# Cached keys turned by VectorE from a block layout that the page gather writes, with each sequence's values moved behind the next sequence's logits

## The chip, the cores and the metric

One core of a Trainium2 chip runs the whole program. The metric is device time in microseconds, of which less is better, as the median of the runs shown.

## What is computed

A two-layer decoder trunk is applied to 512 prompt tokens and to a sample group of 8 sequences with 4 new tokens each, with shared weights. Each layer has one wide input projection, sparse attention, a causal depthwise convolution branch, gates, and an output projection. The change touches only the attention of the sample group. Its cached keys and values lie in pages of 128 tokens; a page table gives 16 pages to each sequence. Cut to that part, for sequence by sequence:

```
k_past = cache_k[l][page_table].reshape(8, 2048, 2, 128)      # 16 pages of 128 tokens, 2 key heads of 128
v_past = cache_v[l][page_table].reshape(8, 2048, 2, 128)
ki_past = cache_kidx[l][page_table].reshape(8, 2048, 64)      # indexer keys, for the top-k choice
s = einsum('btkgd,btnkd->btkgn', q, k_all[idx]) * 128 ** -0.5 # idx: the top 256 keys of each query
o = einsum('btkgn,btnkd->btkgd', softmax(s), v_all[idx])
```

The kernel computes logits against all 2052 keys and adds a bias of -1e30 where a key is not among the top 256, which gives the same result. All data are float32.

## The kernel before

**The frame.** `half_chunk` (L1180) is the frame of everything: per layer 59 column tiles `n` of 256 columns, each in 4 chunks `i` of 512 rows, each chunk in two halves `m`. SP loads a chunk of weights (512 KB) into `raw`, ScalarE makes its high part `w_hi_t` (L882), GpSimd its low part `w_lo_t` (L869), and TensorE (PE) runs 24 float32r products of 272 columns per half. `raw` holds four chunks; SP loads chunk m when GpSimd has finished chunk m - 4.

**The asides.** Everything else is hung behind these halves by tables of step numbers. From tile 11 (`N_GLU`) to tile 42 the steps are numbered h = 0 to 255, one per half, and each engine's `window(l, h)` holds what it does behind that half, in its own program order. The engines meet by semaphores only. The queue of SP is also one program order: `load_weights(m)`, then the `aside` of chunk m - 4, which issues all other transfers.

**The sample attention** starts at h = 200 (`H_AS`) and takes 6 steps (`A_STEP`) per sequence b. With s = 200 + 6b:

- s+0, s+1, s+3, s+4 (`turn_at`): `turn_k` on PE turns a quarter of the keys (4 pages, 512 tokens, 2 heads) by 8 transposes of 128x128 into PSUM (L1377). ScalarE (L1055) and VectorE (`keep_k`, L1848) each copy one head from PSUM into `k_t`. The quarter comes from `k_ring`, a ring of three loads of 512 KB (L633); quarter q may be loaded once quarter q - 3 has been turned.
- s+5 (`logits_at`): `logits_s` multiplies the blocked queries with `k_t` (L1392) and with the new keys (L1395); VectorE (L1854) and ScalarE (L1058) make the softmax.
- s+7 (`pturn_at`): `turn_s` transposes the probabilities (L1402), behind the same half as `turn_k` of the next sequence's second quarter.
- s+8 (`values_at`): `values_s` multiplies them with the values (L1412, L1414) into bank 3 of `aux`; VectorE copies the result out (`keep_o`, L1867). Then SP may load the next sequence's four `v_page` tiles (L638), for which it waits in its queue.

**The gather.** `gather` (L640 to L645) runs in the asides of SP in earlier tiles: it reads a page number into a register and copies that page from the cache to a near DRAM tensor, as it lies, in 16 runs of 8 KB for a page of keys or values. In layer 0, tiles 1 to 16 gather the indexer keys of both layers (two pages per chunk), tiles 17 to 32 the keys and values of layer 0; in layer 1, tiles 1 to 16 gather the keys and values of layer 1. Each k or v page is 128 KB.

Of the kernel before, what the change touches and what calls it, by code (L numbers as in the profile page):

```python
# [5 lines left out]
F32 = mybir.dt.float32  # L6
# [300 lines left out]
def values_at(b):  # L307
    return logits_at(b) + 3
# [28 lines left out]
def trunk_kernel(nc, x_prompt, x_sample, c_prompt, c_sample, cache_k, cache_v, cache_kidx, state_conv, page_table,  # L337
# [4 lines left out]
    with ExitStack() as ctx:  # L342
# [4 lines left out]
        k_near = nc.dram_tensor("k_near", [DEPTH, SEQS, PAGES, PAGE, KVW], F32).ap()  # L347
# [77 lines left out]
        k_ring = at(C + 16512, "k_ring", [P, 3, 4, KVW])  # L425
# [10 lines left out]
        k_t = at(C + 11072, "k_t", [P, 4, KVH, 512])  # L436
# [53 lines left out]
        def ada_place(d):  # L490
# [14 lines left out]
            k_landed0 k_landed1 k_landed2 k_turned k_cp_a k_cp_b logits_s brep_in0 brep_in1 sraw_done exp_s ps_ready pts_ps pts_done  # L505
# [42 lines left out]
        def _(sp):  # L548
# [64 lines left out]
            def load_kx(l, b):  # L613
                if b < 2:
                    sp.wait_ge(S.q_blocked, 2 * l + 1)
                    sp.wait_ge(S.dots_ready, len(PACKS) * (l + 1))
                    sp.wait_ge(S.kx_staged, 16 * DEPTH * SEQS * PAGES)
# [7 lines left out]
            def load_k(l, q):  # L625
# [7 lines left out]
                sp.dma_start(k_ring[:, q % 3], k_near[l, b, 4 * j:4 * j + 4].rearrange("g p c -> p g c")).then_inc(k_landed[q % 3], 16)  # L633
# [6 lines left out]
            def gather(places, staged):  # L640
# [107 lines left out]
            def aside(l, n, i):  # L748
# [7 lines left out]
                kv = [(near[l], cache[l].rearrange("g p h d -> g p (h d)")) for near, cache in ((k_near, cache_k), (v_near, cache_v))]  # L756
# [119 lines left out]
        def _(act):  # L876
# [101 lines left out]
            def window(l, h):  # L978
# [67 lines left out]
                for b in range(SEQS):  # L1046
                    for j in range(4):
                        if h == turn_at(b, j):
                            q = 32 * l + 4 * b + j
                            act.wait_ge(S.k_turned, q + 1)  # L1050
                            if b >= 1:
                                act.wait_ge(S.logits_s, 8 * l + b)
# [1123 lines left out]
```

## Time and profile before

| | |
|---|---|
| median of 3 runs | 3469.86 us (3469.58 to 3471.81) |
| profiled execution | 3463.73 us, span 3461.9 us |
| PE busy | 3381.8 us, 98% of the span |
| VectorE, GpSimd, ScalarE busy | 1828.8, 1238.4, 1047.1 us |
| granted TensorE clock, mean | 0.987 |
| DMA | 593.09 MB, 171 GB/s in the mean |

Busy time of an engine is the time in which the hardware profiler saw it work on an instruction. Matmuls are pipelined: one that starts every 0.25 us is shown with a duration of 0.41 us. The cost of a group of matmuls is therefore read from the starts of its neighbours, not from its own duration. A DMA share is the part of the time in which the core's 16 DMA engines worked on packets.

### The profile page before, as it was taken

The page shows a single profiled execution, that of the slowest core. Times are in us where ns is not written, and L with a number is a line of the kernel's source. Part 1 is how long each engine was busy: PE and PEld are TensorE (multiplying, and loading weights), DVE is VectorE, ACT ScalarE, POOL GpSimd, SP SyncE. Part 2 cuts the span into 40 slices and gives each one's busy share as a digit, 9 for nine tenths or more (in the row PEclk, how much of TensorE's full clock was granted, in tenths as well). Part 3 has the DMA queues.
Part 4 walks back from the last instruction along what each step waited for, and adds up shares of the span by engine and source line. Part 5 has one row for each costly group of instructions (what it writes and reads, how often), then busy time and mean ns, then how long its engine had stood idle before and what let it go on. Part 6 is the DMA issues. An engine that isn't in the chain of part 4 may idle for free. (4 is left out here: it accounts for less than half of the span.)

```text
span 3461.9 us, 66254 instructions
## 1 busy us (share of the span) xinstructions
PE 3381.8 (98%) x27454; PEld 3161.4 (91%) x27454; DVE 1828.8 (53%) x2535; ACT 1047.1 (30%) x1444; POOL 1238.4 (36%) x508
## 2 busy tenths in 40 slices
PE   5899999999999999999999999999999999999999
PEld 2699989989999989998888999898999998899998
DVE  1524468999986123342226244789989841233211
ACT  2322322223542333222223222322235423332211
POOL 0243333446324223333333333334462332234433
PEclk8899999999999999999999999999999999999999
DMA  9844444666545774658895666544332257644444
GB/s 325 283 108 117 109 112 121 188 180 200 155 133 163 232 240 157 210 194 288 289 296 177 182 174 181 141 129 114 102 112 77 84 186 237 219 149 135 131 130 95
DMA packets 591304, 593.09 MB, mean 171 GB/s; under 512 B 110876, under 2 KB 556337, under 8 KB 580923
## 3 DMA queue, kind: packets, MB, share of 16 engines
q1 hardware_dynamic: 588732, 588.59, 56.7%
q8 instruction: 216, 3.54, 0.4%
q14 instruction: 84, 0.69, 0.1%
q10 hardware_dynamic: 2272, 0.28, 0.1%
HBM read 546.37 MB, written 116.39 MB: 191 GB/s over the span
## 5 line engine op out<-in xcount | busy, mean ns | idle before, releaser
L869 POOL TENSOR_TENSOR w_lo_t<-raw,w_hi_t 128x1024 fp32r<-128x1024 f32 x472 | 1193.3, 2529 | 2199.4 <-ACT w_hi_t L882 2199.4
L1180 PE MATMUL acc<-act_hi,w_hi_t 128*128 128x272 f32 x6528 | 1390.0, 294 | 18.2 <-POOL w_lo_t L869 9.7
L1180 PE MATMUL acc<-act_hi,w_lo_t 128*128 128x272 f32 x6528 | 1353.0, 289 | 0.0
L1180 PE MATMUL acc<-act_lo,w_hi_t 128*128 128x272 f32 x6528 | 1349.5, 288 | 0.0
L1180 PEld LDWEIGHTS acc<-act_hi,w_hi_t 128*128 128x128 f32 x6528 | 1028.2, 189 | 77.4 <-issue 55.7
L1180 PEld LDWEIGHTS acc<-act_lo,w_hi_t 128*128 128x128 f32 x6528 | 1028.5, 189 | 0.0
L1180 PEld LDWEIGHTS acc<-act_hi,w_lo_t 128*128 128x128 f32 x6528 | 1022.6, 189 | 0.0
L882 ACT ACTIVATE w_hi_t<-raw 128x1024 fp32r<-128x1024 f32 x472 | 499.9, 1059 | 1645.1 <-PE acc L1180 1631.5
L1757 DVE SCALAR_TENSOR_TENSOR conv<-conv,cw 128x512 f32<-128x512 f32 x240 | 236.1, 984 | 13.6 <-POOL w_lo_t L869 13.6
L1180 PE MATMUL acc<-m_hi,w_hi_t 128*128 128x272 f32 x1024 | 215.2, 292 | 0.0
L1180 PE MATMUL acc<-m_lo,w_hi_t 128*128 128x272 f32 x1024 | 211.5, 287 | 0.0
L1180 PE MATMUL acc<-m_hi,w_lo_t 128*128 128x272 f32 x1024 | 211.4, 287 | 0.0
L1757 DVE SCALAR_TENSOR_TENSOR d_odd<-conv,cw,d_odd 128x512 f32<-128x512 f32 x224 | 196.9, 879 | 12.7 <-POOL w_lo_t L869 12.6
L1658 DVE TENSOR_TENSOR stage<-stage,cs 128x544 f32<-128x544 f32 x38 | 39.5, 1041 | 310.2 <-DMA stage<-stage 310.2
L1848 DVE COPY k_t<-aux 128x512 f32<-128x512 f32 x64 | 44.3, 692 | 242.9 <-PE aux L1377 242.9
L1180 PEld LDWEIGHTS acc<-m_hi,w_hi_t 128*128 128x128 f32 x1024 | 159.6, 188 | 4.1 <-issue 4.1
L1180 PEld LDWEIGHTS acc<-m_lo,w_hi_t 128*128 128x128 f32 x1024 | 161.3, 188 | 0.0
L1180 PEld LDWEIGHTS acc<-m_hi,w_lo_t 128*128 128x128 f32 x1024 | 160.1, 188 | 0.0
L1799 DVE MAX8 top<-work_s 32x8 f32<-32x2052 f32 x62 | 141.5, 2282 | 0.9
L1801 DVE MATCH_REPLACE8 work_s<-top,work_s 32x2052 f32<-32x2052 f32 x62 | 140.6, 2268 | 0.0
L2052 DVE SCALAR_TENSOR_TENSOR x_v<-acc,mod,x_old 128x544 f32<-128x544 f32 x32 | 25.1, 783 | 197.2 <-PE acc L1180 181.0
L2033 DVE TENSOR_TENSOR gates<-acc,gates 128x544 f32<-128x544 f32 x32 | 23.2, 725 | 166.8 <-PE acc L1180 166.8
(244 smaller groups left out, 2599.2 us busy)
## 6 DMA issues: line engine op xcount, KB each, us to landing
raw<-in_w_in_dram SPq DMA_DIRECT2D x272, 512.0 KB, 3.8
ada_ring<-in_w_ada_dram SPq DMA_DIRECT2D x95, 512.0 KB, 7.0
raw<-in_w_in_dram SPq DMA_DIRECT2D x136, 256.0 KB, 3.3
k_near<-in_cache_k_dram SPq DMA_DIRECT2D x256, 128.0 KB, 2.7
v_near<-in_cache_v_dram SPq DMA_DIRECT2D x256, 128.0 KB, 2.7
k_ring<-k_near SPq DMA_DIRECT2D x64, 512.0 KB, 5.2
v_page<-v_near SPq DMA_DIRECT2D x64, 512.0 KB, 6.4
raw<-in_w_out_dram SPq DMA_DIRECT2D x64, 512.0 KB, 4.3
```

The source lines that it names most:

```text
L869: pool.tensor_tensor(w_lo_t[:, m % 2], raw[:, m % 4], w_hi_t[:, m % 2].bitcast(F32), ALU.subtract).then_inc(S.w_lo, 1)
L882: act.activation(w_hi_t[:, m % 2], raw[:, m % 4], ACT.Copy).then_inc(S.w_hi, 1)
L1180: last = pe.matmul(acc[:, 2 * m + h, 0:HALF], w[:, c % 2, k, P * m:P * m + P], r[:, kt, h * HALF:(h + 1) * HALF], start=first and k == 0 a ...
L1658: st.then(dve.tensor_tensor(x, x, cs[:, cos, :], ALU.mult))
L1757: st.then(dve.scalar_tensor_tensor(out=out, in0=src, scalar=w, in1=out, op0=ALU.mult, op1=ALU.add))
L1799: st.then(dve.max(top8[0:NS, :], src))
L1801: st.then(dve.match_replace(work_s[:, :], top8[0:NS, :], src, NEG))
L1848: dve.tensor_copy(k_t[:, j, 1, :], aux[:, 1, :]).then_inc(S.k_cp_b, 1)
L2033: dve.tensor_tensor(pair(gates[:, 2 + m, :]), accv(m), pair(gates[:, 2 + m, :]), ALU.mult).then_inc(acc_free[m], 1)
L2052: st.then(dve.scalar_tensor_tensor(out=pair(x_v[:, k, :]), in0=accv(m), scalar=g[:, 0:1], in1=pair(old), op0=ALU.mult, op1=ALU.add))
```

## The change

- The near key tensor of a page is laid out as (head, block a of 32 dimensions, token, 32 dimensions). The gather writes a key page so, with 1024 pieces of 32 floats (128 bytes), where it copied 16 runs of 8 KB.
- The key pages of each layer are gathered one per chunk in tiles 1 to 32 (`page_at`). Tiles 1 to 16 also gather that layer's own indexer keys, tiles 17 to 32 its values, two pages per chunk. So both layers gather in the same way.
- A load into `k_ring` puts token group k and block a on partition 32a + k, in 1024 pieces of 512 bytes, where it had 512 pieces of 1 KB. One VectorE instruction (`dve.transpose`, 32x32 blocks, 128 partitions by 1024 elements) turns a quarter straight from `k_ring` into `k_t`. The transposes of PE, the two copies out of PSUM and their semaphores go.
- `values_at(b)` becomes `logits_at(b + 1)`, three steps later, behind the same half as the next sequence's logits (for the last one, two steps later). The values are made in bank 0 of `aux`, which the key turns have left; `logits_s` waits no more for `o_done`.

Its core (lines of the changed kernel's neighbours are cut):

```diff
 def values_at(b):
-    return logits_at(b) + 3
+    return logits_at(b + 1) if b < SEQS - 1 else logits_at(b) + 5
...
+def page_at(n, i):
+    return divmod(4 * (n - 1) + i, PAGES)
...
-        k_near = nc.dram_tensor("k_near", [DEPTH, SEQS, PAGES, PAGE, KVW], F32).ap()
+        k_near = nc.dram_tensor("k_near", [DEPTH, SEQS, PAGES, KVH, HD // BLK, PAGE, BLK], F32).ap()
...
-                sp.dma_start(k_ring[:, q % 3], k_near[l, b, 4 * j:4 * j + 4].rearrange("g p c -> p g c")).then_inc(k_landed[q % 3], 16)
+                src = k_near[l, b, 4 * j:4 * j + 4].rearrange("y g a (k m) i -> (a k) (y g) (m i)", m=PAGE // BLK)
+                sp.dma_start(k_ring[:, q % 3], src).then_inc(k_landed[q % 3], 16)
...
+                    if keys is not None:
+                        near, cache = keys
+                        sp.dma_start(near[b, g].rearrange("h a k i -> (h a) k i"),
+                                     cache[ds(page, 1)].rearrange("y k (c i) -> (y c) k i", i=BLK)).then_inc(S.kv_staged, 16)
...
-                if l == 0 and 1 <= n < 17:
-                    gather([(x, [(kx_near[a], cache_kidx[a]) for a in range(DEPTH)]) for x in staged_at(n, i)], S.kx_staged)
-                if l == 0 and 17 <= n < 33:
-                    gather([(x, kv) for x in staged_at(n - 16, i)], S.kv_staged)
-                if l > 0 and 1 <= n < 17:
-                    gather([(x, kv) for x in staged_at(n, i)], S.kv_staged)
+                if 1 <= n < 33:
+                    gather([(page_at(n, i), [])], S.kv_staged, keys)
+                if 1 <= n < 17:
+                    gather([(x, [(kx_near[l], cache_kidx[l])]) for x in staged_at(n, i)], S.kx_staged)
+                if 17 <= n < 33:
+                    gather([(x, [values]) for x in staged_at(n - 16, i)], S.kv_staged)
...
-                            act.activation(k_t[:, j, 0, :], aux[:, 0, :], ACT.Copy).then_inc(S.k_cp_a, 1)
...
-                for g in range(KVH):
-                    for kk in range(4):
-                        last = pe.transpose(aux[:, g, P * kk:P * kk + P], k_ring[:, q % 3, kk, g * HD:(g + 1) * HD], ident)
-                last.then_inc(S.k_turned, 1)
...
-                dve.tensor_copy(k_t[:, j, 1, :], aux[:, 1, :]).then_inc(S.k_cp_b, 1)
+                dve.transpose(k_t[:, j].rearrange("p x (k m) -> p x m k", m=PAGE // BLK),
+                              k_ring[:, q % 3].rearrange("p x (m i) -> p x m i", i=BLK)).then_inc(S.k_turned, 1)
```

**How it moves instructions.** PE, in the sample attention of layer 0, from the second sequence's first key turn to its logits; the rows of the projection (L1180, in the changed kernel L1181) are left out. Before:

```order
L1377 MATMUL aux<-con,k_ring 128x128 [waits k_cp_b,k_cp_a,k_landed1]
...
L1402 MATMUL aux<-con,probs_s 128x128 [waits ps_ready]
...
L1377 MATMUL aux<-con,k_ring 128x128 [waits k_cp_b,k_cp_a,k_landed2]
...
L1412 MATMUL aux<-v_page0,pt_s 32x256 [waits v_landed2,v_landed1,v_landed3,v_landed0,pts_done]
...
L1377 MATMUL aux<-con,k_ring 128x128 [waits k_cp_b,k_cp_a,k_landed0]
...
L1392 MATMUL aux<-k_t,q_blk 32x512 [waits pts_done,q_blocked,o_done,k_cp_b,k_cp_a]
```

The same stretch in the changed kernel:

```order
L1389 MATMUL aux<-con,probs_s 128x128 [waits ps_ready]
L1389 MATMUL aux<-con,probs_s 128x128 x3
L1390 MATMUL aux<-con,p_tail 32x128
...
L1379 MATMUL aux<-k_t,q_blk 32x512 [waits pts_done,q_blocked,k_turned]
L1379 MATMUL aux<-k_t,q_blk 32x512 x7
L1382 MATMUL aux<-k_new,q_blk 32x4 x8
L1401 MATMUL aux<-v_page0,pt_s 32x256 [waits v_landed1,v_landed2,v_landed0,v_landed3,praw_done,pts_done]
```

The four key turns are gone, and the values of the first sequence stand directly behind the logits of the second, with no projection between them.

SP, in the same part of the program, over one sequence. Before:

```order
L633 DMA k_ring<-k_near 128x4x256 [waits k_turned] x2
L638 DMA v_page<-v_near 128x4x256 [waits pv_s,ao_p] x2
L660 DMA gate_spill<-gate 128x544 [waits acc0_free]
L573 DMA raw<-in_w_in_dram 128x4x256 [waits w_lo]
L633 DMA k_ring<-k_near 128x4x256 [waits k_turned]
L638 DMA v_page<-v_near 128x4x256 [waits pv_s,ao_p] x2
```

In the changed kernel:

```order
L639 DMA k_ring<-k_near 128x8x128 [waits k_turned]
L644 DMA v_page<-v_near 128x4x256 [waits pv_s,ao_p] x4
L578 DMA raw<-in_w_in_dram 128x4x256 [waits w_lo]
L665 DMA bias_s<-bias_spill 32x1x512 [waits sraw_done]
L665 DMA bias_s<-bias_spill 32x1x512 x2
L665 DMA bias_s<-bias_spill 32x1x516
L639 DMA k_ring<-k_near 128x8x128 [waits k_turned] x2
```

The four loads of values now go out together, 2 MB ahead of the next weights and of the next two loads of keys.

## Rows read from the trace of the kernel before

**Rows 1.** The page, part 1, and the weight split's row of part 5.

```profile
PE 3381.8 (98%) x27454; PEld 3161.4 (91%) x27454; DVE 1828.8 (53%) x2535; ACT 1047.1 (30%) x1444; POOL 1238.4 (36%) x508
...
L869 POOL TENSOR_TENSOR w_lo_t<-raw,w_hi_t 128x1024 fp32r<-128x1024 f32 x472 | 1193.3, 2529 | 2199.4 <-ACT w_hi_t L882 2199.4
```

**Rows 2.** Groups by line: engine, op, tiles, shapes, count; busy us, mean ns; idle before.

```profile
L1377 PE MATMUL aux<-con,k_ring 128*128 128x128 f32 x512 | 66.3, 273 | 0.0
...
L1848 DVE COPY k_t<-aux 128x512 f32<-128x512 f32 x64 | 44.3, 692 | 242.9 <-PE aux L1377 242.9
...
L2063 DVE STREAM_TRANSPOSE y_t<-x_v 128x512 f32<-128x512 f32 x16 | 11.4, 711 | 0.5
```

**Rows 3.** Timeline of PE around one key turn: start us, duration us, line.

```profile
1154.43 0.41 PE L1180 MATMUL acc<-act_lo,w_hi_t 128*128 128x272 f32 x2
1154.68 0.42 PE L1180 MATMUL acc<-act_hi,w_lo_t 128*128 128x272 f32 x2
1154.93 1.04 PE L1377 MATMUL aux<-con,k_ring 128*128 128x128 f32 x8
1155.72 0.49 PE L1180 MATMUL acc<-act_hi,w_hi_t 128*128 128x272 f32 x2
1156.06 0.42 PE L1180 MATMUL acc<-act_lo,w_hi_t 128*128 128x272 f32 x2
```

**Rows 4.** Timeline of PE around the values of one sequence.

```profile
1175.90 0.41 PE L1180 MATMUL acc<-act_hi,w_lo_t 128*128 128x272 f32 x2
1176.24 1.93 PE L1412 MATMUL aux<-v_page,pt_s 128*32 128x256 f32 x32
...
1178.65 0.52 PE L1180 MATMUL acc<-act_hi,w_hi_t 128*128 128x272 f32 x2
1179.00 0.41 PE L1180 MATMUL acc<-act_lo,w_hi_t 128*128 128x272 f32 x2
```

**Rows 5.** Stretches: length, busy of PE, PEld, DVE, ACT, POOL, granted clock, DMA share, GB/s.

```profile
2821.00:3044.00 223.00, 223.00 (x2032) 201.60 (x2032) 41.80 (x91) 80.45 (x116) 61.72 (x26) 1.00 0.74 236
1169.00:1196.00 27.00, 27.00 (x251) 24.14 (x250) 4.44 (x11) 10.67 (x16) 7.16 (x3) 1.00 0.77 246
1570.00:1770.00 200.00, 198.62 (x1849) 175.49 (x1848) 62.28 (x90) 42.38 (x58) 62.42 (x26) 1.00 0.95 312
```

**Rows 6.** DMA queue in 2685 to 2745 us: packets, MB, share of 16 engines.

```profile
q1 hardware_dynamic: 3600, 4.26, 24.1%
```

**Rows 7.** DMA in 1858 to 1955 us; issues: count, KB each, median us to landing.

```profile
q1 hardware_dynamic: 10620, 17.38, 61.0%
...
k_near<-in_cache_k_dram SPq DMA_DIRECT2D x30, 128.0 KB, 2.8
```

**Rows 8.** DMA in 400 to 573 us.

```profile
q1 hardware_dynamic: 31754, 17.78, 39.0%
...
raw<-in_w_in_dram SPq DMA_DIRECT2D x48, 256.0 KB, 3.3
```

**Rows 9.** DMA in 3256 to 3440 us.

```profile
q1 hardware_dynamic: 47600, 22.49, 45.9%
...
out_dram<-y_t SPq DMA_DIRECT2D x56, 64.0 KB, 2.0
```

**Rows 10.** DMA in 1115 to 1333 us.

```profile
k_ring<-k_near SPq DMA_DIRECT2D x29, 512.0 KB, 4.8
...
raw<-in_w_in_dram SPq DMA_DIRECT2D x25, 512.0 KB, 6.9
```

**Rows 11.** SP's waits in 1115 to 1335 us: us in total, times, longest.

```profile
SPq L573 <- POOL w_lo_t L869: 56.6, 16, 7.4
```

**Rows 12.** Timeline of SP over one weight chunk in layer 1.

```profile
2007.75 0.38 SPq L573 DMA_DIRECT2D raw<-in_w_in_dram  x1
2008.90 0.51 SPq L645 DMA_DIRECT2D k_near<-in_cache_k_dram  x1
...
2013.77 0.38 SPq L573 DMA_DIRECT2D raw<-in_w_in_dram  x1
```

More of the change, by code:

```diff
@@ L435, in trunk_kernel @@
         z_t = at(C + 21176, "z_t", [SEQS, NS])
-        k_t = at(C + 11072, "k_t", [P, 4, KVH, 512])
+        k_t = at(C + 11072, "k_t", [P, 4, 4 * KVH, PAGE])
         bias_s = [at(C + 23456, "bias_s0", [P, 516]), at(C + 15176, "bias_s1", [P, 516])]
@@ L638, in load_v, with gather @@
                 sp.dma_start(v_page[j][:, :, :], v_near[l, b, 4 * j:4 * j + 4].rearrange("g p c -> p g c")).then_inc(v_landed[j], 16)
-            def gather(places, staged):
+            def gather(places, staged, keys=None):
                 for (b, g), targets in places:
@@ L755, in aside @@
                     sp.dma_start(mask_t[:, :, :, :], table[:, T_MASK:N_TAB].rearrange("p (a b n) -> p a b n", a=2, b=SEQS)).then_inc(S.cs_in, 16)
[L756 to L762 removed]
+                keys, values = ((near[l], cache[l].rearrange("g p h d -> g p (h d)")) for near, cache in ((k_near, cache_k), (v_near, cache_v)))
+                if 1 <= n < 33:
[4 more added lines that the diff above has]
+                    gather([(x, [values]) for x in staged_at(n - 16, i)], S.kv_staged)
                 if 1 <= n <= N_GLU and i < 2:
@@ L1046, in window @@
                 for b in range(SEQS):
[L1047 to L1052, printed above, removed]
-                            else:
-                                act.wait_ge(S.bias_stored, 16 * l + 16)
-                            act.activation(k_t[:, j, 0, :], aux[:, 0, :], ACT.Copy).then_inc(S.k_cp_a, 1)
                     if h == logits_at(b):
@@ L1388, in logits_s @@
                     pe.wait_ge(S.pts_done, 8 * l + b)
-                    pe.wait_ge(S.o_done, 8 * l + b)
                 for g in range(KVH):
                     for j in range(4):
-                        pe.matmul(aux[32 * j:32 * j + 32, 2, :], q_blk[:, b, g, :], k_t[:, j, g, :], start=g == 0, stop=g == 1)
+                        pe.matmul(aux[32 * j:32 * j + 32, 2, :].rearrange("p (y n) -> p y n", n=PAGE), q_blk[:, b, g, :], k_t[:, j, g:4 * KVH:KVH, :], start=g == 0, stop=g == 1)
                 for g in range(KVH):
@@ L1457, in window @@
                 for b in range(SEQS):
+                    if h == pturn_at(b):
+                        turn_s(l, b)
+                    if h == logits_at(b):
+                        logits_s(l, b)
+                for b in range(SEQS):
                     if h == values_at(b):
                         values_s(l, b)
-                    if h == pturn_at(b):
-                        turn_s(l, b)
-                    for j in range(4):
-                        if h == turn_at(b, j):
-                            turn_k(l, b, j)
-                    if h == logits_at(b):
-                        logits_s(l, b)
                 if h == H_COMB:
@@ L1840, in turn_q, with turn_k @@
                 last.then_inc(S.q_blocked, 1)
-            def keep_k(l, b, j):
-                dve.wait_ge(S.k_turned, 32 * l + 4 * b + j + 1)
+            def turn_k(l, b, j):
+                q = 32 * l + 4 * b + j
+                dve.wait_ge(k_landed[q % 3], 16 * (q // 3 + 1))
                 if b >= 1:
@@ L1866, in keep_o @@
                 dve.wait_ge(S.pv_s, 8 * l + b + 1)
-                dve.tensor_copy(o_part[b][:, :], aux[:, 3, 136:136 + KVW]).then_inc(S.o_done, 1)
+                dve.tensor_copy(o_part[b][:, :], aux[:, 0, 0:KVW]).then_inc(S.o_done, 1)
             def peaks(l):
@@ L1968, in window @@
                         if h == turn_at(b, j):
-                            keep_k(l, b, j)
+                            turn_k(l, b, j)
+                for b in range(SEQS):
                     if h == values_at(b):
```

22 lines of the change are left out of this document (8 added, 14 removed).

## The prediction

> **What bounds the kernel now.** I read the page first. PE is busy 98% of the span; VectorE, GpSimd and ScalarE have 36 to 53% [rows 1]. Then the stretch of the sample attention in layer 1: PE is busy for all 223 of 223 us, at a granted clock of 1.00, with VectorE at 41.8 us and a DMA share of 0.74 [rows 5]. So what leaves PE's queue there leaves the time, as long as nothing else is late; and the nearest thing to a second bound is DMA, not an engine. The timeline then prices a group of matmuls by its neighbours' starts, and the DMA views price packets by their length.
>
> **What leaves PE.** The projection starts a pair of products every 0.25 us (1154.43 to 1154.68). Around a key turn the last pair before starts at 1154.68, the first two after at 1155.72 and 1156.06 [rows 3]: 1.38 us where two steps of 0.25 would be, so the turn costs 0.88 us, and 0.09 of that is the slow first step when the projection comes back (0.34 for 0.25). There are 4 x 8 x 2 = 64 turns. Fourteen of them (the second quarter of sequences 1 to 7, twice) share their half with the transposes of the probabilities, which stay and keep that 0.09; they give 0.79. The sum is 50 x 0.88 + 14 x 0.79 = **55.1 us**. It can't be more than the 66.3 us that the group shows as busy, since that counts the overlap [rows 2], and hardly less than 64 x 0.70 = 45, if every turn kept an entry and an exit of 0.09.
>
> **The values behind the logits.** The values pay 0.34 for 0.25 before their first matmul and 0.35 for 0.25 behind their last [rows 4]: 0.19 us of switching. Behind the next logits they share that group's entry and exit; the last sequence's share those of the peak transposes. 16 x 0.19 = **3.0 us**; at worst nothing. Their own matmuls stay. `logits_s` loses its wait for `o_done` and the values keep it; PE had no wait here to lose, so this is worth nothing by itself.
>
> **What VectorE takes over.** The nearest row is a block transpose of 128 x 512 at 711 ns [rows 2]; twice that, 1.42 us, is my value for 128 x 1024. The new one writes with a stride, which no row shows; 2.8 us is my upper end, 0.7 the lower. A sequence has 4 of them in place of 4 copies of 0.69: 4 x (1.42 - 0.69) = +2.9 us on 4.44 busy in 27 [rows 5], +8.4 at the upper end. Both are hidden: four turns must fit between two logits, some 23 us apart. VectorE now waits for `k_landed` itself; behind such a wait stand the softmax and the copy of the values, which PE needs one or two halves later. ScalarE loses its copies; nobody waited for them. Nothing of this counts.
>
> **What DMA takes over.** First the price of a byte. With mostly weights in flight, 60 us x 0.241 x 16 engines = 231 engine-us moved 4.26 MB: 54.3 ns per 1000 bytes [rows 6]. With pages going from DRAM to DRAM in 8 KB runs it is 97 x 0.61 x 16 / 17.38 = 54.5, the same [rows 7]. Then the price of a cut. Where the weights come in 24576 pieces of 512 bytes (48 x 256 KB), 173 x 0.39 x 16 = 1080 engine-us stand against 17.78 x 54.3 = 965: 4.6 ns more per piece [rows 8]. Where the outputs go in 28672 pieces of 128 bytes (56 x 64 KB), it is 1351 against 1221: 4.5 ns [rows 9].
>
> - A load of keys: 28.5 engine-us for its bytes, plus 1024 x 4.6 = 4.7: 2.07 us of the 16 engines where it had 1.78. A sequence needs 0.77 x 27.0 = 20.8 us of DMA now [rows 5], then 20.8 + 4 x 0.29 = 22.0. Its PE time falls to 27.0 - 3.5 - 0.2 = 23.3. The share rises to 94%. That is much, but a stretch with a share of 0.95 has PE at 198.6 of 200 us [rows 5]. Cost: nothing.
> - A gathered key page: 7.1 + 4.7 = 11.8 engine-us, 0.74 us in place of 0.45. No row shows 128-byte pieces from DRAM to DRAM; I take rows 9 and use as upper end a 1 KB packet's price, 55.6 ns per piece, so 3.6 us per page. A chunk lasts 6.02 us [rows 12] and needs 1.78 for weights, 0.74 for the page and 0.2 for two indexer pages, or 0.9 for two value pages: under 3.5 us, and 5.6 to 6.2 at the upper end, where the chunks of tiles 17 to 32 also hold asides of PE. Cost: nothing, with room up to (6.0 - 2.0) x 16 / 1024 = 62 ns per piece.
> - SP's queue: a gathered copy takes 0.51 us and the reading of a page number about 0.77 (2008.13 to 2008.90); a chunk of 6.02 us held two readings and four copies [rows 12], 3.6 us. Now it is three and three, 3.8 us. In the sample attention SP still stood 56.6 us waiting for weights to be split [rows 11], so it is not late.
> - The burst: four value loads (7.1 us), a chunk of weights (1.8), bias rows (under 1) and then the fourth quarter of the keys (2.1), which would land some 13 to 14 us after the preceding values; its turn is needed after six halves, 6 x 3.0 + 0.7 = 18.8 us. It fits by about 4 us. The weights have four chunks of ring, some 20 us, against landings of 6.9 us [rows 10].
>
> **Sum.** -55.1 - 3.0 = -58.1 us. The profiled execution has 3463.73 us and becomes 3405.6; it is 6.1 below the median of the runs shown, so the median becomes 3469.9 - 58.1 = **3411.8 us**, 1.7% less. The likeliest case's own ends are 3408 (a little more of the switching goes) and 3422 (the low end of the turns).
>
> **Rival 1: DMA becomes the bound of the sample attention.** It decides once a sequence needs more than 23.3 us, so once a 512-byte piece costs over (28.5 + 0.62 x 16) / 1024 = 37.5 ns, against 32.4 by rows 8. For it: only 14% of margin, weight landings of 6.9 us there [rows 10] where the halves of a chunk took 3.3 earlier [rows 8], and the burst. Against it: the 0.95 stretch. Halfway, at 24.8 us per sequence, 16 x 1.5 = 24 us are lost: 3436. At the full price of a 1 KB packet a load takes 3.56 us and a sequence 27.9: slower than now by 16 x 0.9 = 14 us, 3484.
>
> **Rival 2: the gather in 128-byte pieces is too dear.** This is the slower side. It decides from 62 ns per piece. At twice a 1 KB packet's price, 111 ns, a page takes 7.1 us and a chunk 9.1, where the chunks last 3462 / 472 = 7.3 us in the mean [rows 1]; over 256 chunks that is +460 us, about 3870. Against it: stores of 128-byte pieces cost 11.5 ns each [rows 9]. For it: those go from SBUF, while here both ends are DRAM and the reads jump by 1 KB. The Trainium skill (DMA: Bandwidth & Descriptors, Specifications) says that below 512 bytes a transfer is done as read-modify-write; that would be such a mechanism, though on the stores of rows 9 no such price is seen.
>
> **Rival 3: the copy falls apart into single floats.** If a rearranged copy were moved element by element, 32 packets of 4.6 ns and the bytes make 154 ns per piece, 9.9 us per page, 11.9 per chunk, +1180 us: 4590. Against it: both sides have runs of 32 floats, and the weights' cut to 512 bytes cost a piece's price, not an element's. The Trainium skill (VectorE: DVE Perf Modes, The three transpose paths) warns that a plain copy whose access pattern makes the transpose is 19 times slower when the innermost destination stride is large. Here the innermost stride is one element, so I read the rule as not meeting this case; 19 times 0.45 us would be 8.5 us per page.
>
> **Chances.** Forecast 0.78, rival 1 0.14 (mostly between 3420 and 3450), rival 2 0.06, rival 3 0.01, anything else 0.01. A measurement of this kernel tells about 0.2% (7 us) from no change. Faster by more than that: the forecast and most of rival 1, 0.90. Within it: a part of rival 1, 0.03. Slower: rivals 2 and 3 and the far end of 1, 0.07. The range 3407 to 3440 holds the forecast with its ends and the nearer half of rival 1.
>
> **What would show it.** In the changed profile the group of key transposes is absent, PE is still busy for all of the sample attention, a sequence takes 23.3 us (that stretch 26 to 28 us shorter per layer), the other stretches last as long as before, and the DMA share there is about 0.9. The block transposes show 1.3 to 1.5 us; over 3 the estimate is wrong, over 4 PE waits for them. Rival 1 would show waits of PE for `k_t`, `v_page` or `w_lo_t` there and a share near 1. Rivals 2 and 3 would show the chunks of tiles 1 to 32 longer than before, with PE waiting for weights. A gain under 45 us with no new wait would mean that I misprice a turn.

## The result and the profile after

The changed kernel takes 3446.57 us (median of 4 runs, 3442.52 to 3450.13) against 3470.84 us for the kernel before on the same chip. The ratio is 0.9927, 95% interval [0.9912, 0.9943]: 24 us faster, where 58 were forecast, and outside the range given. The profiled execution has 3449.85 us, span 3448.0. That is 3.3 us above its median, and the profiled execution before was 7.1 below its own (3463.73, span 3461.9), so the two traces differ by 13.9 us where the medians differ by 24.3. What follows on single stretches is from the traces.

First the page of the changed kernel (parts 1 and 5), beside [rows 1] and [rows 2].

```profile
PE 3342.3 (97%) x26942; PEld 3116.9 (90%) x26942; DVE 1919.6 (56%) x2535; ACT 1012.8 (29%) x1380; POOL 1241.7 (36%) x508
...
L1181 PE MATMUL acc<-act_hi,w_hi_t 128*128 128x272 f32 x6528 | 1388.2, 294 | 37.8 <-POOL w_lo_t L879 14.1
...
L1645 DVE TENSOR_TENSOR stage<-stage,cs 128x544 f32<-128x544 f32 x38 | 41.1, 1082 | 336.2 <-DMA stage<-stage 336.2
...
L1837 DVE STREAM_TRANSPOSE k_t<-k_ring 128x1024 f32<-128x1024 f32 x64 | 124.6, 2021 | 135.3 <-DMA k_ring<-k_near 135.0
```

The 512 transposes are gone from PE. But PE's idle time ahead of the projection is 37.8 us; here is the same row of the kernel before:

```profile
L1180 PE MATMUL acc<-act_hi,w_hi_t 128*128 128x272 f32 x6528 | 1390.0, 294 | 18.2 <-POOL w_lo_t L869 9.7
```

**Where the gain is.** Windows of the changed kernel, with the columns of [rows 5]; the last two lie in the sample attention of layer 0 and of layer 1, the first in tile 5 and the second in tile 12 of layer 0.

```profile
246.00:260.00 14.00, 10.84 (x74) 10.43 (x73) 6.00 (x6) 2.19 (x3) 4.91 (x2) 0.90 0.47 114
...
437.00:468.00 31.00, 28.55 (x200) 27.79 (x201) 14.91 (x28) 5.47 (x6) 9.25 (x4) 0.83 0.51 132
1162.00:1260.00 98.00, 98.00 (x910) 87.20 (x909) 41.23 (x45) 32.04 (x45) 30.86 (x13) 1.00 0.91 269
2866.00:2960.00 94.00, 94.00 (x878) 83.20 (x878) 37.91 (x43) 30.42 (x41) 28.73 (x12) 1.00 0.92 267
```

In the sample attention PE is busy for all of the time at a granted clock of 1.00, and DMA has a share of 0.91 to 0.92: as forecast. The first two windows are of another kind. Before, they read as follows; the second lies there in tiles 12 and 13, since the kernel before reaches tile 12 at 424.5 us already and has PE busy for all of its 26.8 us.

```profile
246.00:260.00 14.00, 14.00 (x114) 14.00 (x113) 0.83 (x1) 3.26 (x4) 6.77 (x3) 1.00 0.45 114
...
437.00:468.00 31.00, 31.00 (x246) 29.92 (x245) 17.19 (x29) 7.61 (x9) 13.13 (x5) 1.00 0.45 116
```

**The map of the time.** GpSimd's 472 splits of weights (`w_lo_t`) are a clock of the program: the time from the first split of one tile to the first of a later tile is the length of the tiles between. In us, from the profiled executions (layer 0 / layer 1):

| tiles | before | after | e1 | e3 | e2 |
|---|---|---|---|---|---|
| 5 | 24.1 / 24.1 | 29.2 / 29.2 | 24.1 / 24.1 | 24.1 / 24.1 | 24.1 / 24.1 |
| 6 | 25.9 / 25.9 | 30.7 / 28.1 | 25.9 / 25.9 | 25.9 / 25.9 | 25.9 / 25.9 |
| 7 to 10 | 102.8 / 102.8 | 104.8 / 104.8 | 102.8 / 102.8 | 102.8 / 102.8 | 102.8 / 102.8 |
| 11 to 16 | 174.8 / 174.8 | 183.4 / 183.1 | 174.8 / 174.8 | 174.8 / 174.8 | 174.8 / 174.8 |
| 19 to 26 | 222.6 / 224.1 | 226.3 / 225.1 | 222.6 / 224.1 | 223.6 / 225.3 | 226.4 / 229.9 |
| 27 to 30 | 122.2 / 122.2 | 122.2 / 122.2 | 122.2 / 122.2 | 122.2 / 122.2 | 127.8 / 129.4 |
| 33 to 42 | 311.7 / 311.5 | 283.1 / 282.7 | 283.0 / 283.0 | 282.9 / 283.7 | 283.2 / 283.5 |

Tiles 33 to 42 hold the sample attention: 28.6 and 28.8 us shorter, 57.4 together. Tiles 5 to 26 are 24.2 and 18.6 us longer, 42.8 together. So the gain is there in full, and in these traces three quarters of it are given back somewhere else, in tiles whose work on PE the change doesn't touch (by the medians, 34 of the 58 us that were forecast). Within tiles 11 to 16 the whole loss lies in tile 12, which takes 35.4 and 35.1 us in place of 26.8. Tiles 43 to 57 (not in the table) vary by up to 4.5 us between the kernels.

**What PE waits for there.** PE's waits in 148 to 1010 us of the changed kernel: us in total, times, longest.

```profile
PE acc L1181 <- ACT stage L919: 4.8, 3, 2.8
PE aux L1250 <- DVE q_att L1654: 4.5, 1, 4.5
PE acc L1181 <- POOL w_lo_t L879: 3.8, 2, 2.9
PE acc L1181 <- ACT stage L922: 3.0, 1, 3.0
```

Before, in the same stretch:

```profile
PE acc L1180 <- ACT gate L945: 2.0, 3, 1.1
PE acc L1180 <- POOL w_lo_t L869: 1.9, 1, 1.9
```

`stage` and `q_att` are rotated queries and keys. Their rows are first exchanged by four small DMA copies (`stage<-stage`), which SP issues at the end of its aside. The timeline shows the chain: VectorE waits for the copies, then ScalarE copies out of `acc`, then PE may write `acc` again. VectorE, ScalarE and PE of the changed kernel; the first three rows have their idle time in brackets:

```profile
253.76 0.81 DVE L1645 TENSOR_TENSOR stage<-stage,cs 128x544 f32<-128x544 f32 x1 [3.90 <-DMA stage<-stage]
...
256.06 0.62 ACT L919 ACTIVATE stage<-acc 128x544 f32<-128x544 f32 x1 [4.54 <-DVE qi L1656]
...
256.74 0.52 PE L1181 MATMUL acc<-act_hi,w_hi_t 128*128 128x272 f32 x2 [2.78 <-ACT stage L919]
257.09 0.62 PE L1181 MATMUL acc<-act_lo,w_hi_t 128*128 128x272 f32 x2
...
258.41 0.66 PE L1181 MATMUL acc<-act_lo,w_hi_t 128*128 128x272 f32 x2
258.87 0.66 PE L1181 MATMUL acc<-act_hi,w_lo_t 128*128 128x272 f32 x2
```

The last rows show a second price. Behind the wait of 2.78 us a pair starts every 0.45 us (258.41 to 258.87) in place of 0.25: the window has a granted clock of 0.90 in the mean, so part of it is at 1.2 GHz. After the wait of 4.51 us that ends at 439.45 us the pairs from 444.11 to 448.19 us start 0.45 us apart as well. Two narrower windows have nothing but the lower clock (0.50, so 1.2 GHz):

```profile
257.13:260.53 3.40, 3.40 (x18) 3.40 (x17) 0.00 (x0) 0.00 (x0) 0.00 (x0) 0.50 0.48 112
438.03:448.26 10.23, 8.81 (x42) 8.08 (x43) 4.19 (x10) 1.28 (x1) 0.47 (x1) 0.50 0.48 117
```

In tiles 5 to 26 of the changed kernel there are seven such stretches, four in layer 0 and three in layer 1, each begun in a wait of 2.8 to 4.5 us or within 2 us of its end, with 33.9 us of busy PE in them; before there was one, beside a wait of 1.8 us, with 3.4 us. 30.5 us at 0.45 per pair in place of 0.25 lose some 14 us. PE's idle time in these tiles grew by 26.8 us (5.8 to 32.6; over the whole span 105.7 us, 3448.0 - 3342.3, where it had 80.1). Together that is 40 of the 42.8 us.

**What makes the copies late.** The timeline of SP, which issues them, over one chunk with exchanges, changed kernel:

```profile
271.57 0.44 SPq L578 DMA_DIRECT2D raw<-in_w_in_dram  x1
272.99 0.78 SPq L654 DMA_DIRECT2D k_near<-in_cache_k_dram  x1
275.04 1.86 SPq L651 DMA_DIRECT2D kx_near<-in_cache_kidx_dram  x2
276.95 2.83 SPq L616 DMA_DIRECT2D stage<-stage  x4
279.82 0.44 SPq L578 DMA_DIRECT2D raw<-in_w_in_dram  x1
```

And before:

```profile
232.91 0.44 SPq L573 DMA_DIRECT2D raw<-in_w_in_dram  x1
234.31 3.27 SPq L645 DMA_DIRECT2D kx_near<-in_cache_kidx_dram  x4
237.62 2.81 SPq L611 DMA_DIRECT2D stage<-stage  x4
240.48 0.44 SPq L573 DMA_DIRECT2D raw<-in_w_in_dram  x1
```

A chunk with exchanges keeps SP for 8.25 us instead of 7.57, with no idle time in it. Over the chunks without exchanges that start in 150 to 250 us the median, from one issue of weights to the next, is 5.4 against 4.7. In tiles 1 to 5 two chunks of a tile have four exchange copies and two have none: SP needs 2 x (8.3 + 5.4) = 27.4 us per tile, where PE needs 24.1 to 24.3. Before it was 2 x (7.61 + 4.72) = 24.7, so SP was already all but full there, and the page, which has no busy time for SP, doesn't show it.

These medians leave out one price of the small pieces. In each layer, the issue of the `kx_near` copy right behind the second key page takes SP 3.8 us where the others take some 0.5 (the row has two issues and the reading between them):

```profile
163.56 5.11 SPq L651 DMA_DIRECT2D kx_near<-in_cache_kidx_dram  x2
```

The same happens, at the same place, in every kernel that copies key pages in small pieces in tiles 1 to 16 (2.7 to 3.9 us in e1, e5, e7, e8, e9) and in none of the others (before, e2, e3, e4, e6). Why, no run shows.

The Trainium skill (Perfetto Trace Analysis, What "DMA-bound" means) names the DMA sequencer of the issuing engine as one of the things that can bind, and says that its track is then solid DMA slices. The first half holds here. The second doesn't quite: between the slices of SP above there are gaps of up to 1.3 us (273.77 to 275.04) in which it waited for nothing that the profile shows; the reading of a page number lies in each of them.

### The profile page after: what moved, and what is told of

Same layout as the page of the kernel before. It is cut to its first block and busy times, and to the rows that moved or that the text cites. A ratio compares the mean times of both kernels' runs of the same rounds, so it can differ in the third digit from the quotient of the medians.

```text
span 3448.0 us, 66432 instructions
## 1 busy us (share of the span) xinstructions
PE 3342.3 (97%) x26942; PEld 3116.9 (90%) x26942; DVE 1919.6 (56%) x2535; ACT 1012.8 (29%) x1380; POOL 1241.7 (36%) x508
## 5 line engine op out<-in xcount | busy, mean ns | idle before, releaser
L1181 PE MATMUL acc<-act_hi,w_hi_t 128*128 128x272 f32 x6528 | 1388.2, 294 | 37.8 <-POOL w_lo_t L879 14.1
L1181 PE MATMUL acc<-act_hi,w_lo_t 128*128 128x272 f32 x6528 | 1357.2, 289 | 0.0
L1181 PE MATMUL acc<-act_lo,w_hi_t 128*128 128x272 f32 x6528 | 1353.2, 289 | 0.0
L1181 PEld LDWEIGHTS acc<-act_hi,w_hi_t 128*128 128x128 f32 x6528 | 1033.0, 189 | 98.8 <-issue 57.8
L1181 PEld LDWEIGHTS acc<-act_lo,w_hi_t 128*128 128x128 f32 x6528 | 1032.0, 190 | 0.0
L1181 PEld LDWEIGHTS acc<-act_hi,w_lo_t 128*128 128x128 f32 x6528 | 1026.6, 190 | 0.0
L1181 PE MATMUL acc<-m_hi,w_hi_t 128*128 128x272 f32 x1024 | 215.8, 292 | 0.0
L1181 PE MATMUL acc<-m_lo,w_hi_t 128*128 128x272 f32 x1024 | 212.0, 288 | 0.0
L1181 PE MATMUL acc<-m_hi,w_lo_t 128*128 128x272 f32 x1024 | 211.6, 288 | 0.0
L1837 DVE STREAM_TRANSPOSE k_t<-k_ring 128x1024 f32<-128x1024 f32 x64 | 124.6, 2021 | 135.3 <-DMA k_ring<-k_near 135.0
L1181 PEld LDWEIGHTS acc<-m_hi,w_hi_t 128*128 128x128 f32 x1024 | 160.0, 188 | 4.5 <-issue 3.7
L1181 PEld LDWEIGHTS acc<-m_lo,w_hi_t 128*128 128x128 f32 x1024 | 161.8, 189 | 0.0
L1181 PEld LDWEIGHTS acc<-m_hi,w_lo_t 128*128 128x128 f32 x1024 | 160.5, 188 | 0.0
```

Of the source, the lines that this page charges most:

```text
L1181: last = pe.matmul(acc[:, 2 * m + h, 0:HALF], w[:, c % 2, k, P * m:P * m + P], r[:, kt, h * HALF:(h + 1) * HALF], start=first and k == 0 a ...
L1837: dve.transpose(k_t[:, j].rearrange("p x (k m) -> p x m k", m=PAGE // BLK), k_ring[:, q % 3].rearrange("p x (m i) -> p x m i", i=BLK)).the ...
```

## The experiments

Two theories. **S**: SP's queue is full in tiles 1 to 11; the new gather gives it three readings of page numbers per chunk instead of two, and key copies that are dear to issue. **P**: the 128-byte pieces are dear to the DMA engines, and SP's own time doesn't matter.

**e1: one reading less.** The key page is copied behind a reading that the chunk makes anyhow. All copies stay as they are.

```diff
-                    if keys is not None:
+                    if keys is not None and y in which:
...
-                if 1 <= n < 33:
-                    gather([(page_at(n, i), [])], S.kv_staged, keys)
...
-                    gather([(x, [(kx_near[l], cache_kidx[l])]) for x in staged_at(n, i)], S.kx_staged)
+                    gather([(x, [(kx_near[l], cache_kidx[l])]) for x in staged_at(n, i)], S.kx_staged, keys, (0,))
...
-                    gather([(x, [values]) for x in staged_at(n - 16, i)], S.kv_staged)
+                    gather([(x, [values]) for x in staged_at(n - 16, i)], S.kv_staged, keys, (1,))
```

> The changed kernel, with two page numbers read per chunk in place of three: the key page of a chunk is the first of the two indexer pages (tiles 1 to 16) or the second of the two value pages (tiles 17 to 32), and uses the number that is read for it anyway. Copies, sizes and the 128-byte pieces stay. Theory S (SP's own issue time bounds tiles 1 to 16, the third reading tips it, and late swap copies stop PE): the chunks of tiles 5 to 16 go back to 6.0 to 7.3 us, the waits of PE for ACT stage and DVE q_att there vanish, and the median falls by about 35 to 40 us to 3405 to 3415. Theory P (the 128-byte pieces hold the DMA engines up): the pieces are the same, so the time stays within 3440 to 3450.

Measured: 3408.37 us, ratio 0.9833 [0.9819, 0.9846], with span 3403.2. The two windows above are full again (as before, the one at 437 us lies in tiles 12 and 13):

```profile
437.00:468.00 31.00, 31.00 (x246) 29.92 (x245) 17.16 (x30) 7.37 (x9) 13.15 (x5) 1.00 0.54 129
246.00:260.00 14.00, 14.00 (x114) 14.00 (x113) 0.00 (x0) 3.26 (x4) 6.72 (x3) 1.00 0.51 119
```

The 43 us lost in tiles 5 to 26 are back (table above) with the same pieces and the same bytes, and the DMA share of these windows is higher than in the changed kernel. SP's median chunk is 4.8 us without exchanges and 7.65 with four. This is the best version found, and it beats both kernels.

**e2: the old timetable of the gather with the new layout.** Layer 0 gathers both layers' indexer pages in tiles 1 to 16, and tiles 17 to 32 of both layers gather two pages of keys and values per chunk.

```diff
-                    sp.wait_ge(S.kx_staged, 16 * SEQS * PAGES * (l + 1))
+                    sp.wait_ge(S.kx_staged, 16 * DEPTH * SEQS * PAGES)
...
-                if 1 <= n < 33:
-                    gather([(page_at(n, i), [])], S.kv_staged, keys)
-                if 1 <= n < 17:
-                    gather([(x, [(kx_near[l], cache_kidx[l])]) for x in staged_at(n, i)], S.kx_staged)
+                if l == 0 and 1 <= n < 17:
+                    gather([(x, [(kx_near[a], cache_kidx[a]) for a in range(DEPTH)]) for x in staged_at(n, i)], S.kx_staged)
...
-                    gather([(x, [values]) for x in staged_at(n - 16, i)], S.kv_staged)
+                    gather([(x, [values]) for x in staged_at(n - 16, i)], S.kv_staged, keys)
```

> The changed kernel with the old timetable: indexer pages of both layers in layer 0, tiles 1 to 16; keys (in blocks) and values, two pages of each per chunk, in tiles 17 to 32 of both layers; nothing gathered in tiles 1 to 16 of layer 1. Theory S: no swap copies are issued in tiles 17 to 32, so the longer issue there costs nothing; 3405 to 3415. Theory P: twice as many 128-byte pieces per chunk in tiles 17 to 32 cost at least as much as before, 3440 or more, with the loss moved to tiles 17 to 32.

Measured: 3430.30 us, ratio 0.9892 [0.9876, 0.9908], between the ranges that the two theories had named: S had expected no loss here, and was wrong in that. The early tiles lose nothing (table). The loss is now in tiles 19 to 30, 9.5 us in layer 0 and 13.0 in layer 1 against before. SP of this kernel over one chunk there:

```profile
824.41 0.42 SPq L578 DMA_DIRECT2D raw<-in_w_in_dram  x1
826.10 0.54 SPq L651 DMA_DIRECT2D v_near<-in_cache_v_dram  x1
826.74 0.77 SPq L654 DMA_DIRECT2D k_near<-in_cache_k_dram  x1
828.78 0.55 SPq L651 DMA_DIRECT2D v_near<-in_cache_v_dram  x1
829.42 0.76 SPq L654 DMA_DIRECT2D k_near<-in_cache_k_dram  x1
830.25 1.10 SPq L670 DMA_DIRECT2D gate_spill<-gate  x1
831.40 0.42 SPq L578 DMA_DIRECT2D raw<-in_w_in_dram  x1
```

7.0 us for a chunk, and SP waits for the weights to be split only 17.2 us in 600 to 1010 us, where before it waited 114.2. In layer 0 these tiles have the readings and copies of the kernel before, two and four per chunk; only the pieces of the key pages are smaller. The loss goes where SP is asked to do most. That fits S, without its belief that only tiles with exchange copies can lose; it fits P too, since the pieces moved with it. It was e3 to e6 that took these apart.

**e3: large pieces, the same readings.** The key page is copied as it lies, in the changed kernel's places; the keys then stand in `k_near` in another order.

```diff
-                        sp.dma_start(near[b, g].rearrange("h a k i -> (h a) k i"),
-                                     cache[ds(page, 1)].rearrange("y k (c i) -> (y c) k i", i=BLK)).then_inc(S.kv_staged, 16)
+                        sp.dma_start(near[b, g:g + 1].rearrange("y h a k i -> y (h a k i)").rearrange("y (k c) -> y k c", c=KVW),
+                                     cache[ds(page, 1)]).then_inc(S.kv_staged, 16)
```

> The changed kernel with the key pages copied as they lie, in long runs, so the near keys are in the wrong order and the sample attention works on wrong keys; the timetable and the three readings per chunk stay. Theory S: only the issue of the key copy gets shorter, 0.51 us in place of 0.78, of the 0.8 us that a chunk has too much; a third of the loss goes, 3430 to 3440. Theory P: the whole loss goes, 3405 to 3412.

Measured: 3411.29 us, ratio 0.984 [0.9825, 0.9855]. The whole loss of tiles 5 to 16 is gone, more than S had said, and as P had said; P seems to win. SP's timeline in this kernel shows why it does not:

```profile
220.49 0.58 SPq L578 DMA_DIRECT2D raw<-in_w_in_dram  x1
221.82 0.51 SPq L654 DMA_DIRECT2D k_near<-in_cache_k_dram  x1
223.09 1.76 SPq L651 DMA_DIRECT2D kx_near<-in_cache_kidx_dram  x2
224.89 0.58 SPq L578 DMA_DIRECT2D raw<-in_w_in_dram  x1
```

The issue takes 0.51 us in place of 0.78, and from its end to the next copy 0.76 us pass (222.33 to 223.09) in place of 1.27 (273.77 to 275.04). The small pieces cost SP 0.27 + 0.51 = 0.78 us per key page, and SP's chunk falls to 4.6 us. I had priced the pieces on the DMA engines and not on the issuer.

**e4: the kernel before with one more reading.** A reading of a page number that nothing uses, in each chunk of tiles 1 to 16.

```diff
+                if 1 <= n < 17:
+                    sp.value_load(pages[0:1, 4 * n + i:4 * n + i + 1], min_val=0, max_val=n_phys - 1)
```

> The kernel before with one more page number read into a register per chunk in tiles 1 to 16 of both layers, used by nothing; no copy is added. Theory S: the same loss appears in tiles 5 to 16, slower by 25 to 50 us, about 3495 to 3520, with PE waiting for ACT stage. Theory P: a reading is no DMA load worth naming, so 3470, unchanged.

Measured: 3480.93 us, ratio 1.0043 [1.0028, 1.0059]: 15 us slower, where S had expected 25 to 50. SP's chunks grow to 5.2 and 8.1 us in layer 0, which loses 14.0 us: tile 6 takes 29.5 us, tile 7 27.1 (before 25.2), and tiles 11 to 16 take 183.3, all of their loss in tile 12. In layer 1 they are 5.1 and 8.0 us, and the loss is 2.0 us (tiles 7 to 10). So without any small piece, 0.5 us more of SP's time per chunk brings a loss in the same tiles, smaller than that of the changed kernel.

**e5: e1 with one more reading.** The two lines of e4, added to e1.

> The variant with shared readings, and in tiles 1 to 16 of both layers one more page number read into a register that nothing uses. It then has SP's three readings and three copies of the changed kernel again, and everything else of the fast variant. Theory S: the loss comes back, 3438 to 3450, in the same tiles (5 to 16). Rival R (what sharing removed was not SP's time but something else of the changed timetable, such as which page is gathered when): 3405 to 3412.

Measured: 3443.71 us, ratio 0.9924 [0.9909, 0.9939]. The 35 us are lost again, in the same tiles in both layers (tile 6 30.5, tiles 11 to 16 183.5 and 183.1), with SP's chunks at 5.3 and 8.2 us. The copies are those of e1, piece by piece. This settles it against P: e1 has all the small pieces and no loss, and one reading more brings it.

**e6: e3 with one more reading.** The same two lines, added to e3.

> The changed timetable with the key pages copied as they lie (wrong key order), and one more unused page number read per chunk in tiles 1 to 16. There are no 128-byte pieces at all. A chunk then takes SP about 4.4 + 0.75 = 5.15 us without swaps, nearly the 5.3 of the changed kernel. Theory S: 3430 to 3445, the loss is back without a single small piece. Theory P: 3408 to 3413, as without the reading.

Measured: 3417.67 us, ratio 0.9851 [0.9836, 0.9866], 6 us above e3 where 19 or more were expected; the intervals of the two overlap, so the time alone tells no difference. SP's chunks are 5.1 and 8.0 us, a little shorter than those of e4 and e5, and the trace has a part of the loss: 2.0 us in tiles 7 to 10 of each layer, nothing in tile 6 and nothing in tile 12. Tiles 19 to 26 of layer 0 are 4.8 us longer than before, but the added reading isn't in them, and in layer 1 they are 1.5 shorter. Neither theory's range was met.

SP's need per tile in tiles 1 to 5, as 2 x (chunk without + chunk with exchanges), puts most of these in order. Chunks are medians from one issue of weights to the next, of those that start in 150 to 250 us (layer 0) or 1860 to 1960 us (layer 1). The loss is the sum over tiles 5 to 16 against before; the last column is how long after the first weight split of tile 12 VectorE has written the last `q_att` that PE needs there (minus: ahead of it).

| kernel, layer | SP per tile, us | loss, us | last `q_att`, us |
|---|---|---|---|
| e3, 0 | 24.3 | 0.0 | -3.0 |
| before, 0 | 24.7 | 0 | -2.8 |
| e1, 0 | 24.9 | 0.0 | -2.5 |
| e4, 1 | 26.2 | 2.0 | -1.9 |
| e6, 1 | 26.2 | 2.0 | -1.7 |
| e6, 0 | 26.3 | 1.9 | -1.7 |
| e4, 0 | 26.8 | 14.0 | 3.2 |
| e5, 0 | 26.9 | 17.2 | 3.2 |
| after, 1 | 27.1 | 17.6 | 3.2 |
| e5, 1 | 27.3 | 16.7 | 3.2 |
| after, 0 | 27.4 | 20.5 | 3.2 |
| e9, 0 | 27.9 | 10.2 | -1.5 |
| e9, 1 | 28.0 | 16.3 | 3.1 |

The loss is no straight line in SP's need: a queue that is too slow by 2 us in each of five tiles still costs only 2 us in all, and from 26.3 to 26.8 us the loss jumps to 14. My reading of the first part, which no run tested by itself, is that the ring of four chunks (a tile's worth of weights) gives the queue room until it is used up.

The jump is mostly tile 12, which takes either 26.8 us or 35.0 to 35.5, and the traces show how late exchange copies grow on VectorE. Two instructions of VectorE's chain and the two weight splits of GpSimd beside them, changed kernel:

```profile
423.42 2.90 DVE L1646 TENSOR_TENSOR stage<-stage,cs 128x544 f32<-128x544 f32 x1
430.58 2.56 DVE L1654 TENSOR_TENSOR q_att<-stage 128x544 f32<-128x544 f32 x1
...
423.22 2.51 POOL L879 TENSOR_TENSOR w_lo_t<-raw,w_hi_t 128x1024 fp32r<-128x1024 f32 x1 [4.56 <-ACT w_hi_t L892]
430.16 2.40 POOL L879 TENSOR_TENSOR w_lo_t<-raw,w_hi_t 128x1024 fp32r<-128x1024 f32 x1 [4.42 <-ACT w_hi_t L892]
```

Before, the same two instructions take their usual 0.72 us, and the splits (at 411.52 and 418.45 us) fall beside VectorE's reciprocals:

```profile
409.14 0.72 DVE L1659 TENSOR_TENSOR stage<-stage,cs 128x544 f32<-128x544 f32 x1
414.11 0.72 DVE L1667 TENSOR_TENSOR q_att<-stage 128x544 f32<-128x544 f32 x1
```

In every kernel, each instruction of this kind in tiles 1 to 12 that took over 1.3 us overlaps a weight split (some that overlap one stay short). So copies that come some 3 us late move VectorE's chain onto two splits, and these hold it back by some 4 us more: PE then waits 4.4 to 4.5 us for `q_att` in each of the six layers that lose in tile 12. That the split is what holds VectorE is read from the times; no run moved a split.

SP's waits for the weight split in 148 to 350 us are the slack that SP has left. Before, in e1, and in the changed kernel:

```profile
SPq L573 <- POOL w_lo_t L869: 22.8, 11, 5.6
```

```profile
SPq L578 <- POOL w_lo_t L877: 16.3, 8, 5.6
```

```profile
SPq L578 <- POOL w_lo_t L879: 5.6, 1, 5.6
```

**e7: the values at their old step.** e1 with `values_at(b)` as it was.

```diff
-    return logits_at(b + 1) if b < SEQS - 1 else logits_at(b) + 5
+    return logits_at(b) + 3
```

> The variant with shared readings, with the values back at three steps behind the logits, alone behind their half. By the prediction's term of 0.19 us for 16 groups the time is 3.0 us longer than that of the variant, 3411; if the merging is worth nothing, the same; if the V loads in one burst had cost something, up to 5 us shorter.

Measured: 3413.68 us, ratio 0.9844 [0.9831, 0.9858]; the interval overlaps that of e1. In the traces tiles 33 to 42 take 283.5 us in both layers in place of 283.0. PE's own starts tell more. In e7 the values take 3.11 us from the last pair before them to the second behind them (1169.97 to 1173.08) and the logits 2.65 (1181.59 to 1184.24); together, behind one half of the changed kernel, they take 4.95 (1176.72 to 1181.67). Less the 0.50 of two pairs that is counted twice, that saves 0.31 us for each of 7 sequences per layer, 4.3 in all. Against it stands one wait of PE for split weights in these tiles, of 0.85 us per layer in e1 and none in e7. That leaves 2.6 us. The turns alone are 28.2 and 28.0 us (311.7 and 311.5 less 283.5, both kernels without idle time of PE there).

**e8: a dense output of the turn.** e1, with `k_t` written without the stride, so that its keys are in another order.

```diff
-                dve.transpose(k_t[:, j].rearrange("p x (k m) -> p x m k", m=PAGE // BLK),
-                              k_ring[:, q % 3].rearrange("p x (m i) -> p x m i", i=BLK)).then_inc(S.k_turned, 1)
+                dve.transpose(k_t[:, j].rearrange("p x n -> p (x n)"),
+                              k_ring[:, q % 3].rearrange("p x n -> p (x n)")).then_inc(S.k_turned, 1)
```

> The variant with shared readings, with the block transpose writing its output densely, so the keys come to lie in the wrong order in k_t and the sample attention is wrong. If the stride of the output is what makes a turn 2.02 us, it falls to 1.3 to 1.42 us (711 ns for 512 columns); if not, it stays at 2.0. The time of the kernel stays at 3408 in both cases, since PE does not wait for a turn.

Measured: 3411.41 us, ratio 0.9835 [0.982, 0.985], the same as e1. The turn's row:

```profile
L1835 DVE STREAM_TRANSPOSE k_t<-k_ring 128x1024 f32<-128x1024 f32 x64 | 76.6, 1228 | 162.6 <-DMA k_ring<-k_near 162.3
```

The stride of 16 bytes in the output costs 0.8 us of 2.0, and it is hidden. The dense turn is a little below the 1.3 to 1.42 us that were expected.

**e9: the exchanges first.** The changed kernel, with the exchange copies issued ahead of the chunk's gather.

```diff
+                if 1 <= n <= N_GLU and i < 2:
+                    swap_rows(l, n - 1, i)
...
-                if 1 <= n <= N_GLU and i < 2:
-                    swap_rows(l, n - 1, i)
```

> The changed kernel with the copies that exchange rows (stage from stage, four per chunk) issued by SP ahead of the chunk's reading and page copies instead of behind them; the same instructions in number, so SP's time per chunk with exchanges stays near 8.3 us, above the 6 us and more that a tile's chunks leave for it on average. Theory S (what is late is the exchange copies, because SP reaches them late): they go out 4 to 5 us earlier within each chunk, the waits of PE on ScalarE's stage and VectorE's q_att shrink, but SP's total work is still too much for the short tiles, so the lateness only moves to the next chunk's raw weights: a part of the loss goes, 3415 to 3440. Theory Q (SP's total alone counts, order does not): 3443 to 3450, with PE waiting on POOL's raw weights instead. Theory P (the price is the DMA engines', not SP's): no change, 3443 to 3450, with the waits where they were.

Measured: 3445.6 us (3435.45 to 3448.13), ratio 0.9935 [0.9918, 0.9952]: not to be told from the changed kernel. The profiled execution was the shortest of the four, and there the loss in tiles 5 to 26 is 27.2 us in place of 42.8. Tiles 11 to 16 of layer 0 take 174.9 us, but in layer 1 they take 183.0, and tile 6 of layer 0 takes 31.7. SP's chunks with exchanges are no shorter (8.7 us at the median, 8.3 expected). The median lies in the range that Q (SP's total counts and its order doesn't) and P shared. But Q had expected PE to wait for weights instead, and PE's new waits are still for `stage` and `q_att` (4.0 us the longest in layer 0, 4.4 in layer 1); so the run confirms neither. What it shows is that the order does something: layer 0 has more need of SP than any kernel above it in the table and half the loss, since its chain on VectorE misses the splits and tile 12 takes 26.9 us. How much the order alone is worth stays open; it does not cure the loss.

## Why the prediction was wrong

**The turns (-55.1): right.** Tiles 33 to 42 became 56.2 us shorter without the move of the values (e7), so pricing a group by its neighbours' starts held to 2%. The rest is in the 14 turns beside the probabilities: such a half takes 1.92 us before and 1.05 without the turn, so they gave 0.87 each and not 0.79.

**The values (-3.0): right as far as the runs tell.** 0.31 us per merged sequence in place of my 0.19, less a new wait of 0.85 per layer that I did not foresee: 2.6 us. The medians of e1 and e7 can't tell it from nothing. The sum of both terms, 58.1, stands against 57.4 measured.

**VectorE's turn (1.42 us, 0.7 to 2.8): too low, hidden as said.** 2.02 us. The nearest row had a dense output, and e8 shows that the dense turn takes 1.23 us: my doubling was 0.19 too high for it, and the stride adds 0.79.

**DMA in the sample attention (share 94%): right.** 0.91 to 0.92, with PE full. The landings of the keys grew from 4.8 to 7.7 us, and PE waited for none; its only wait in tiles 33 to 42 was one for split weights, 0.9 us in layer 0 and 0.6 in layer 1. Rival 1 did not happen beyond that.

**The price of a piece (4.6 ns, page 11.8 engine-us): a little low.** DMA queue in 1855 to 1952 us, e1 and then e3, which differ in the key pieces:

```profile
q1 hardware_dynamic: 25782, 11.49, 49.4%
```

```profile
q1 hardware_dynamic: 10176, 11.77, 43.4%
```

6.0% of 97 x 16 engine-us are 93, and 15 more for the 0.28 MB that e1 moved less there: 108 engine-us over 15606 packets, 6.9 ns each. A page is then 14 engine-us, 0.9 us. The Trainium skill (DMA: Bandwidth & Descriptors, Specifications) says that transfers below 512 bytes are done as read-modify-write. Whether these pieces were, no run shows; all that they cost from DRAM to DRAM is these 6.9 ns, against the 4.5 of the stores of [rows 9]. Rivals 2 and 3 did not happen: 6.9 ns are far from the 62 from which rival 2 decides, and with the same pieces e1 has none of the loss. (Rival 3's 8.5 us per page took 19 times the copy as it lies; the figure that it cites compares two ways to transpose, so those 8.5 us had no basis. Measured is twice.)

**SP's queue ("3.8 us instead of 3.6 ... so it is not late"): the step that failed.** It had three faults, and the runs put a size on each.

- I read SP's slack in the wrong stretch. The 56.6 us of [rows 11] are from the sample attention, and [rows 12] is a chunk of layer 1 without exchanges. The place where SP does most is tiles 1 to 11, and I never summed a chunk there. The sum was to be had from the trace of before: 4.7 and 7.6 us, 24.7 us per tile against 24.3.
- I left out two things that the same queue does: the issue of the weights (0.44 us at 271.57) and the exchange copies (2.8 us).
- I took the new copy at the old copy's 0.51 us, and its 1024 pieces for the DMA engines' matter alone. It takes 0.78 us, and the reading behind it 0.5 us more. So the chunk grew by 0.7 us and not by 0.2: my 0.2 would have given 24.7 + 4 x 0.2 = 25.5 us per tile, by the table above hardly a loss.

The forecast had no rival in which the issuing queue is late. "Tiles 1 to 32 longer than before" stood among the signs of rivals 2 and 3, and so their sign appeared without their cause.

**How a small excess becomes 43 us.** In three steps that the prediction had nothing of. Late exchange copies shift VectorE's chain, in tile 12 onto two weight splits, which about doubles the lateness. PE waits, 26.8 us more than before in tiles 5 to 26. And behind waits of 2.8 to 4.5 us there it has stretches of 3.4 to 10.2 us at a granted clock of 0.50, which cost some 14 us more.

Tiles 19 to 26 vary by 1 to 5 us between the kernels other than e2 (226.3 in the changed kernel and in e7, 222.6 in e1) with the same gather in e1 and e7. The traces show what the difference is made of: PE's idle time there is 1.8 to 3.8 us, most of it one wait for split weights of 1.8 or 2.9 us, and each stretch of 3.4 us at a granted clock of 0.50 adds 1.5. e1 in layer 0 has 1.8 us and no such stretch, e7 has 3.8 us and one. What decides between them is open; a wait of 2.9 us had no such stretch behind it in layer 0 of e3 and of e8.

## What to carry to other kernels

Before a transfer is moved, cut finer or given a reading of its own, sum all that its issuing queue does in one chunk, in the busiest stretch that it is moved to, from the timeline of that queue, and hold it against the time that PE takes for the chunk: the page shows no busy time for SP, and its waits are the slack that can be read. Where the excess is small, look at what the delayed engine runs into: the lateness can grow there. A copy's number of pieces is a price of the issuer as well as of the DMA engines. And where a pure gain on PE comes out short, measure each stretch of the program by a regular event: the gain and its loss may lie in different stretches.

## What the runs showed of the hardware

- Issuing a copy of 1024 pieces of 128 bytes took SP 0.78 us, the same bytes in large pieces 0.51 us, and the time from its end to the next copy, with the reading of a register in it, 1.27 us in place of 0.76. The price comes on two rows, and the second one carries the name of the next copy.
- The issue right behind the second such copy of each layer took 2.7 to 3.9 us, in all six kernels that had them in tiles 1 to 16, and in none of the five others.
- A reading of a register that nothing uses costs SP about 0.5 us per chunk (e4, e5, e6). It cost 35 us of kernel time in e5 against e1, 15 in e4 against before, and at most some 6 in e6 against e3, which is not clear of noise.
- An instruction of VectorE with two inputs of 128 x 544 float32 took 0.72 us, and 2.0 to 2.9 us where it ran beside one of GpSimd's weight splits in tiles 11 and 12 of the changed kernel.
- A block transpose of 128 x 1024 float32 on VectorE takes 1.23 us with a dense output and 2.02 us with elements 16 bytes apart.
- After waits of 2.8 us (ended at 256.74 us) and 4.5 us (ended at 439.45) PE started pairs every 0.45 us in place of 0.25, with a granted clock of 0.50 over 257.13 to 260.53 and 438.03 to 448.26 us.
